# Retention heads inside the stick-breaking steps, roots by logarithm and exponential

## The reference, cut to what matters

```python
# block 2, retention: scores by a fixed decay, then a group norm per head and a gate
scores = einsum('bnihd,bnjhd->bnhij', qc, kc) * decay_intra
y_ret = head_group_norm(y_ret, ret_norm_gain) * silu(r_g)
# (yf - mu) * rsqrt(var + EPS), per head of 64, times gain
# block 2, stick-breaking
log_beta = log_sigmoid(z)
log_stay = where(mask, log_beta - z, 0.0)
log_w = log_beta + cumsum(log_stay, axis=3, reverse=True) - log_stay
w = where(mask, exp(log_w), 0.0);  y = einsum('bhqs,bhsd->bhqd', w, v)
mixed = concatenate([y_ret, rms_norm(y_sb)]) @ w_out
# peer
act = gelu(einsum('pd,ped->pe', xb, u[ids])) * gate
y = einsum('pe,ped->pd', act, v[ids])
```

## Time and profile before

| | us |
|---|---|
| median of 3 runs | 3147.92 (3145.39 to 3149.68) |
| the profiled execution | 3149.68 |
| its span | 3147.8 |
| PE busy | 3022.7 (96%) |
| DVE busy | 2420.9 (77%) |
| ACT busy | 1351.2 (43%) |
| POOL busy | 1356.0 (43%) |
| mean granted clock of PE | 0.982 |
| DMA | 931.22 MB, 296 GB/s mean |

### The profile page before, as it was taken

One profiled execution on the slowest core, in us unless ns is written; L12 is line 12 of the kernel. 1 busy time (PEld: TensorE's weight loads), 2 busy tenths in 40 slices (PEclk: granted clock), 3 DMA queues, 4 the chain that ended last, 5 costly groups with the idle time before them and its releaser, 6 DMA issues. The chain is left out here.

```text
span 3147.8 us, 45955 instructions
## 1 busy us (share of the span) xinstructions
PE 3022.7 (96%) x16392; PEld 2028.0 (64%) x16392; DVE 2420.9 (77%) x5361; ACT 1351.2 (43%) x3429; POOL 1356.0 (43%) x1066
## 2 busy tenths in 40 slices
PE   8999999899999999999999988998999999999998
PEld 3467488766666666666444564887666666666664
DVE  6885369989899888867733274699898998888777
ACT  3332222786666555510111172227866665555100
POOL 0000000767676776765300010006576767767654
PEclk9999999999999999999999999999999999999999
DMA  9511352999999999999822201619899999999998
GB/s 309 201 54 37 126 206 74 368 330 409 408 408 396 407 409 409 409 409 409 342 92 87 76 18 56 225 62 354 321 409 408 409 400 406 409 409 409 409 409 346
DMA packets 283115, 931.22 MB, mean 296 GB/s; under 512 B 31853, under 2 KB 32509, under 8 KB 282505
## 3 DMA queue, kind: packets, MB, share of 16 engines
q0 software_dynamic: 147840, 536.96, 43.3%
q1 hardware_dynamic: 135048, 391.34, 32.7%
HBM read 921.87 MB, written 6.32 MB: 295 GB/s over the span
## 5 line engine op out<-in xcount | busy, mean ns | idle before, releaser
L816 PE MATMUL psum<-hT,mod 128*128 128x256 f32 x4096 | 961.1, 389 | 7.3 <-ACT big L1364 6.3
L816 PEld LDWEIGHTS psum<-hT,mod 128*128 128x128 f32 x4096 | 777.4, 194 | 126.4 <-issue 26.1
L1374 ACT ACTIVATE levels<-key_numbers,hT 128x128 bf16<-128x128 f32 x1792 | 567.0, 389 | 245.8 <-PE psum L872 241.9
L2127 DVE SCALAR_TENSOR_TENSOR tmp<-w,small,tmp 128x1024 f32<-128x1024 f32 x339 | 435.7, 1285 | 92.6 <-DMA w<-in_peer_v,tmp 44.1
L2107 DVE CUSTOM_DVE_ANT_0 w<-w,hn 128x1024 f32<-128x1024 f32 x342 | 408.6, 1223 | 74.9 <-DMA w<-in_peer_down,tmp 39.0
L2307 POOL DMA_INDIRECT w<-in_peer_u,tmp x172 | 236.8, 1377 | 521.7 <-DVEq L1892 402.7
L826 PE MATMUL psum<-rows,big 128*128 128x512 f32 x752 | 337.1, 592 | 0.0
L872 PEld LDWEIGHTS psum<-x,levels 128*128 128x128 bf16 x6144 | 226.9, 103 | 165.9 <-issue 127.3
L1377 ACT ACTIVATE levels<-levels 128x512 bf16<-128x512 bf16 x448 | 282.3, 630 | 14.2
L2307 POOL DMA_INDIRECT w<-in_peer_down,tmp x170 | 235.2, 1384 | 119.5 <-DVE small L2107 78.0
L872 PE MATMUL psum<-x,levels 128*128 128x32 bf16 x6144 | 235.8, 196 | 52.4 <-DVE levels L1982 21.6
(11 more groups left out here) (358 smaller groups left out, 4205.6 us busy)
## 6 DMA issues: line engine op xcount, KB each, us to landing
mod<-in_uT SPq DMA_DIRECT2D x256, 512.0 KB
rows<-in_peer_v SPq DMA_DIRECT2D x64, 512.0 KB
rows<-in_peer_up SPq DMA_DIRECT2D x64, 512.0 KB
w<-in_w_in SPq DMA_DIRECT2D x14, 2048.0 KB, 8.0
srow<-in_peer_v SPq DMA_DIRECT2D x32, 512.0 KB, 7.1
tmp<-in_peer_v SPq DMA_DIRECT2D x32, 512.0 KB
srow<-in_peer_up SPq DMA_DIRECT2D x32, 512.0 KB, 6.8
tmp<-in_peer_up SPq DMA_DIRECT2D x32, 512.0 KB
```

Of the source, the lines that this page charges most:

```text
L816: last = nc.tensor.matmul(ps[4 + e % 2][:, 0:ND], ub[e % UV][:, k, :], hT[:, k, ND:SEQ], start=k == 0, stop=k == KC - 1)
L1374: last = nc.scalar.activation(hits[n % HITS][:, j * P:(j + 1) * P], keyno, ACT.Abs, bias=nibT[:, n * BATCH + j:n * BATCH + j + 1])
L2127: last = stt(y, row, c8[g % 2][:, b:b + 1], y, ALU.mult, ALU.add)
```

## The change

Three heads of retention (`AHEAD_HEADS`) stay ahead of the steps; the other five run inside the first 20: a step issues one key tile's scores after the stick scores, DVE multiplies by the decay at the end of its step, and PE sums a head's values at every fourth step. Their scores have two banks instead of four; retention's values and the sticks' share one bank, half each, with waits for its reading. Odd heads' keys get tiles of their own (`rk_odd`) whose other half POOL sets to zero. Weights and stays are stored as triangles, in `hT_`, `w_` and `top_`; for that reason SP loads the second half of w_out after the last step's sums, and the next section after the sticks' values and the scaling. Retention's norm goes by pairs of heads (`centred` at steps 1, 7, 15 and 23, squares, sums, one root at 27, `ret_normed` from 28 to 31, `gated` partly behind the steps); the gate times the gain is POOL's. A stick head's values are read one step earlier. One modulation product of 128x1024 on DVE moves from between retention heads to step 13. Every root is now `Exp(-0.5 * Ln(var))` without a reciprocal, and the table set that has both functions is loaded by name where it may be missing (the start, inside and after block 1's heads, after its late chunks, two places of its expert loop, and block 2 ahead of the first turns and of the steps). In the expert loops of both blocks `unit_gelu` stands ahead of `block_gelu` and `hit_batch`.

```diff
+AHEAD_HEADS = 3
...
+        rk_odd = [v.rearrange("p (g n) -> p g n", g=2) for v in (rows[:, 0, :], part(modm, 20, 4))]
...
-        stay = [part(big, 8 * n, 8).rearrange("p (j n) -> p j n", j=NT) for n in range(2)]
+        def triangle(base, at):
+            widths = [SEQ - j * P for j in range(NT)]
+            return [base[:, at + sum(widths[:j]):at + sum(widths[:j + 1])] for j in range(NT)]
+        stay = [triangle(w_, 1280 * n) for n in range(2)]
+        weights = [triangle(hT_, 1280 * n) for n in range(2)]
+        ret = [triangle(hT_, 2560), [top_[:, 0:512], top_[:, 512:896], w_[:, 3328:3584], w_[:, 3584:3712]]]
...
-        key_sums = [part(rows[:, 0, :], 2 * n, 1.5).rearrange("p (m n) -> p m n", m=3) for n in range(2)]
...
+            sp.wait_ge(ar_done, STICKS)
             load_section(25)
-            sp.wait_ge(pv_used, 8 + 16)
+            sp.wait_ge(pv_used, 8 + 8)
+            sp.wait_ge(src_ready, 9 * NT)
...
+            def ret_score(h, j):
+                n = h * NT + j
+                if n >= 2:
+                    pe.wait_ge(wt_ready, n - 1)
+                keys = rk_odd[h // 4][:, h // 2 % 2, :] if h % 2 else rkT[:, h // 2, :]
+                nc.tensor.matmul(ps[2 + n % 2][:, 0:SEQ - j * P], keys[:, j * P:(j + 1) * P], rqT[:, h // 2, j * P:SEQ],
+                                 start=True, stop=True).then_inc(ret_scored, 1)
+            def ret_values(h):
+                pe.wait_ge(wt_ready, (h + 1) * NT)
+                if h:
+                    pe.wait_ge(ret_used, h)
+                if h > AHEAD_HEADS:
+                    pe.wait_ge(pv_used, 8 + h - AHEAD_HEADS)
+                head_values(ps[0][:, 256:512], ret[h % 2], lambda j: rv[:, j, h * 64:(h + 1) * 64], ret_done)
+            pe.wait_ge(others_zeroed, 3)
+            for h in range(AHEAD_HEADS):
                 for j in range(NT):
-                    n = h * NT + j
-                    if n >= 4:
-                        pe.wait_ge(wt_ready, n - 3)
-                    nc.tensor.matmul(ps[4 + n % 4][:, 0:SEQ - j * P], rkT[prt, h // 2, j * P:(j + 1) * P],
-                                     rqT[prt, h // 2, j * P:SEQ], start=True, stop=True).then_inc(z_done, 1)
-                if h >= 1:
-                    pe.wait_ge(wt_ready, h * NT)
-                    values(h - 1, st1[(h - 1) % 2], lambda j: rv[:, j, (h - 1) * 64:h * 64], 64, first=h == 1)
-            pe.wait_ge(wt_ready, 8 * NT)
-            values(7, st1[1], lambda j: rv[:, j, 448:512], 64)
+                    ret_score(h, j)
+                if h:
+                    ret_values(h - 1)
...
+                if AHEAD_HEADS * NT + n < 8 * NT:
+                    ret_score(AHEAD_HEADS + n // NT, n % NT)
...
+                if n % NT == 1 and AHEAD_HEADS - 1 + n // NT < 8:
+                    ret_values(AHEAD_HEADS - 1 + n // NT)
...
-                nc.scalar.activation(std[:, at:at + n], var[:, at:at + n], ACT.Sqrt).then_inc(std_ready, 1)
+                root_step(nc.scalar.activation(lnv[:, at:at + n], var[:, at:at + n], ACT.Ln))
+                nc.scalar.activation(rs[:, at:at + n], lnv[:, at:at + n], ACT.Exp, scale=-0.5).then_inc(rs_ready, 1)
...
+                    nc.scalar.preload_act_table_set("natural_log_exp_and_others")
...
+                    for u in range(units_due(e - 2), units_due(e - 1)):
+                        unit_gelu(layer, u)
                     if EARLY <= e + AHEAD - 1 < NKEY:
                         block_gelu(layer, e + AHEAD - 1)
                     for n in range(batches_due(e) if e else 0, batches_due(e + 1)):
                         hit_batch(layer, 1 + n // BATCHES, n % BATCHES)
-                    for u in range(units_due(e - 2), units_due(e - 1)):
-                        unit_gelu(layer, u)
...
+                nc.scalar.activation(rk_odd[0][64:P, :, t * P:(t + 1) * P], bank[64:P, 0:2], ACT.Copy)
+                nc.scalar.activation(rk_odd[1][64:P, :, t * P:(t + 1) * P], bank[64:P, 2:4], ACT.Copy).then_inc(tr_free[n % 2], 1)
...
+            def ret_out(h):
+                act.wait_ge(ret_done, h + 1)
+                nc.scalar.activation(hn[:, :, h * 64:(h + 1) * 64], ps[0][:, 256:512].rearrange("p (t n) -> p t n", t=NT), ACT.Copy)\
+                    .then_inc(ret_used, 1)
...
-                if n in (2, 5, 8, 11):
+                if n in (1, 8, 16, 24):
+                    p = n // 8
                     seen.next(dve_to_act)
-                    act.wait_ge(heads_summed, 8 + n // 3)
-                    nc.scalar.activation(wide_sq, hn[:, n // 3, 0:512], ACT.Square).then_inc(ss_done, 1)
-                if n == 14:
+                    if p:
+                        act.wait_ge(ret_summed, p)
+                    nc.scalar.activation(wide_sq.rearrange("p (t n) -> p t n", t=NT), hn[:, :, p * P:(p + 1) * P], ACT.Square)\
+                        .then_inc(ss_done, 1)
+                if n == 26:
                     root(8 * NT)
-                    nc.scalar.preload_act_table_set("natural_log_exp_and_others")
...
-                    if j == 0 and h >= 1:
-                        head_out(h - 1, 64, 512, 8 + 8 + h, stick_sq[(h - 1) % 2], 8 + 4 + h - 2 if h >= 3 else 0)
-            head_out(7, 64, 512, 8 + 8 + 8, stick_sq[1], 8 + 4 + 6)
-            act.wait_ge(pv_used, 8 + 16)
+                    if j == 1 and h >= 1:
+                        head_out(h - 1, 64, 512, 8 + h, stick_sq[(h - 1) % 2], 8 + h - 2 if h >= 3 else 0)
+                if n % NT == 2 and AHEAD_HEADS - 1 + n // NT < 8:
+                    ret_out(AHEAD_HEADS - 1 + n // NT)
...
-                seen.next(std_ready)
-                step(nc.vector.reciprocal(rs[:, c], std[:, c]))
+                seen.next(rs_ready)
...
+            def ret_weights(h, j):
+                n = h * NT + j
+                if j == 0:
+                    dve.wait_ge(dec_in[h % 2], 16 * (h // 2 + 1))
+                    if h >= 2:
+                        dve.wait_ge(ret_done, h - 1)
+                dve.wait_ge(ret_scored, n + 1)
+                wd = SEQ - j * P
+                tt(ret[h % 2][j], ps[2 + n % 2][:, 0:wd], dec[h % 2][:, 0:wd], ALU.mult).then_inc(wt_ready, 1)
+            for h in range(AHEAD_HEADS):
+                for j in range(NT):
+                    ret_weights(h, j)
+            def centred(p):
+                pair = hn[:, :, p * P:(p + 1) * P].rearrange("p t (h n) -> p t h n", n=64)
+                mean = nt_[:, 0:8].rearrange("p (t h) -> p t h", h=2)
+                dve.wait_ge(ret_used, 2 * p + 2)
+                step(nc.vector.tensor_reduce(mean, pair, AX_X, ALU.add))
+                step(ts(nt_[:, 0:8], nt_[:, 0:8], 1.0 / 64, None, ALU.mult))
+                tt(pair, pair, mean.unsqueeze(3).to_broadcast([P, NT, 2, 64]), ALU.subtract).then_inc(dve_to_act, 1)
+            def ret_normed(t):
+                rv_, rshape = by_head(hn[:, t, 0:512], 8, 64)
+                step(tt(rv_, rv_, spread(rs[:, 8 * t:8 * t + 8], rshape), ALU.mult))
+            def gated(t):
+                dve.wait_ge(rg_ready, t + 1)
+                step(tt(hn[:, t, 0:512], hn[:, t, 0:512], rg[:, t, :], ALU.mult))
...
+            for n in range(STICKS + LOOK + 1):
+                if n in (1, 7, 15, 23):
+                    centred((n + 1) // 8)
+                if n in (2, 9, 17, 25):
+                    p = n // 8
+                    seen.next(ss_done)
+                    nc.vector.tensor_reduce(ss.rearrange("p (t h) -> p t h", t=NT)[:, :, 2 * p:2 * p + 2],
+                                            wide_sq.rearrange("p (t h n) -> p t h n", t=NT, n=64), AX_X, ALU.add).then_inc(ret_summed, 1)
+                if n == 13:
                     dve.wait_ge(mod_in, 16)
                     step(stt(rows[:, 1, :], mod[:, 4, :], 1.0, rows[:, 1, :], ALU.add, ALU.mult))
-                dve.wait_ge(dec_in[h % 2], 16 * (h // 2 + 1))
-                if h >= 2:
-                    dve.wait_ge(pv_done, 8 + h - 1)
-                for j in range(NT):
-                    n = h * NT + j
-                    dve.wait_ge(z_done, n + 1)
-                    wd = SEQ - j * P
-                    tt(st1[h % 2][:, j, j * P:SEQ], ps[4 + n % 4][:, 0:wd], dec[h % 2][:, 0:wd], ALU.mult).then_inc(wt_ready, 1)
-            def centred(t):
-                rv_, rshape = by_head(hn[:, t, 0:512], 8, 64)
-                mean = nt_[:, 0:8]
-                step(nc.vector.tensor_reduce(mean, rv_, AX_X, ALU.add))
-                step(ts(mean, mean, 1.0 / 64, None, ALU.mult))
-                tt(rv_, rv_, spread(mean, rshape), ALU.subtract).then_inc(dve_to_act, 1)
-                step(tt(rg[:, t, :], rg[:, t, :], srow[:, 0:512], ALU.mult))
-            def gated(t):
-                rv_, rshape = by_head(hn[:, t, 0:512], 8, 64)
-                step(tt(rv_, rv_, spread(rs[:, 8 * t:8 * t + 8], rshape), ALU.mult))
-                step(tt(hn[:, t, 0:512], hn[:, t, 0:512], rg[:, t, :], ALU.mult))
...
-            for n in range(STICKS + LOOK + 1):
```

(33 more changed lines are left out.)

83 lines of the change are left out of this document (50 added, 33 removed).

## The result

The changed kernel takes 3130.78 us (median of 6 runs, 3129.23 to 3134.83) against 3146.05 for the kernel before on the same chip (6 runs, 3144.53 to 3149.68): a ratio of 0.995, interval 0.994 to 0.996, some 15 us less. Forecast were 3136 us and a range of 3126 to 3147. The profiled execution has a span of 3128.7 us against 3147.8; of those 19.1 us some 4 belong to the profiled execution of before, which lay 3.6 us above its median.

What follows compares the result with a forecast made beforehand. Expert streams were taken as bound by bytes and matmul columns, retention by PE, the steps by PE, DVE and ACT together. Terms -26.9 + 14.0 - 1.9 + 1.3 + 0.5 + 1.0 gave -12.0 us: 3136 us, range 3126 to 3147.

Steps and rivals of the forecast that it cites:

- The stretch: Block 2, end of projections to first turn of the mixed tiles: ahead phase, steps and tail together, forecast -14.8 us.
- Ahead: Retention before the stick-breaking steps: three heads' scores and two heads' values stay, 12.3 us for 39.2, so -26.9 us.
- Steps: Stick-breaking steps with five heads' scores and six heads' values moved in: 93.6 us against 79.6, so +14.0 us.
- Tail: After the last sums: root loses table load and reciprocal, gains an activation, copies come earlier; -1.9 us.
- PE's 15.2 us of idle time: Old steps: 79.6 us less 64.4 of pure PE price, taken as idle; 1.5 + 3.5 us expected to stay.
- The first rival: Merged steps: the chain through DVE and ACT sets their pace, +8 us, 3144 us; chance 0.16.
- The 2.2 us a set: Merged steps: PE price per retention set of 1280 columns, engine taken as warm; 11 sets, 24.2 us.
- Block 1: Table set loaded by name between last late projection and first turn, where PE waits for ACT: +1.3 us.
- The two activations ahead of the queries: Start of both query phases, where PE waits for a root's chain: two activations for one, +0.5 us for both.
- The unit gelu: Expert loops: gathered unit's gelu ahead of the block gelu that PE waits for; +1 us, bounds -2.5 to +6.
- The third rival: Expert streams: unit gelu first frees gathered rows sooner, queues recover; 6 us a block, -24 in all, 3124 us; chance 0.05.
- The second, slower rival: Expert streams: PE's 10.4 us lost to the unit gelu are given back in neither block, +7.8, 3156 us; chance 0.08.

Runs made afterwards that it cites:

- experiment 6: Changed kernel with square root and reciprocal put back for every root, named table loads out; the stretch took 118.61 us against 115.98.
- experiment 3: Changed kernel with all eight retention heads ahead of the steps; 3136.08 us, ratio 0.9962, the stretch 120.39 us against 115.98.
- experiment 5: Changed kernel with eight heads ahead and retention's norm by pairs at the old kernel's steps; the stretch took 126.04 us against 120.39 with the new timetable.
- experiment 7: Kernel before with only the roots changed to exponential and logarithm; the stretch took 129.19 us against 131.29, one whole execution 3148.89 us.
- experiment 2: Kernel before with only the unit gelu moved ahead of block gelu and hit_batch; 3145.1 us, ratio 0.9991.
- experiment 8: Changed kernel with the gate times the gain back on DVE, none on POOL; the stretch took 115.99 us against 115.98.
- experiment 9: Changed kernel with block 1's table load moved from before the first turn to behind the second turned tile; 3132.39 us, ratio 0.9948.
- experiment 1: Changed kernel with the unit gelu put back behind block gelu and hit_batch in both expert loops; 3137.69 us, ratio 0.9969.
- experiment 11: Changed kernel with the unit gelu between block gelu and hit_batch in both expert loops; 3134.03 us, ratio 0.9954.
- experiment 12: Changed kernel with two heads ahead, six inside, centring at steps 4, 12, 20, 27, root at 31; the stretch took 116.36 us against 115.98.

## Why the prediction was right, and where it was not

The stretch was forecast to lose 14.8 us and lost 15.3. *Ahead*: 12.3 us said, 13.0 measured from the first retention score (1774.10) to the first stick score; the two banks cost short waits of 0.2 to 0.3 us each, and no wait on the decay tile came. *Steps*: 93.6 said, 93.54 measured, PE's work 88.6 said, 89.84 measured; as long as retention's scores ran the gaps were 0.24 us where 1.5 were allowed, behind them 3.5 (37.21 less 33.75), as allowed. So 1.2 us more work and 1.3 us less waiting cancel, which is luck. *Tail*: -1.9 said, -3.2 measured. The root's share is right to 0.1 us (experiment 6), the earlier copies gave 0.64 where 0.5 was said (a wait of 1.44 for 2.08 ahead of the last value product); the rest is that product, 1.2 us shorter by the clock, a term the sum did not have and luck in this execution. Without it the stretch loses 14.1.

The sum was right, and the reason for its largest term was not. It let retention's heads fill PE's 15.2 us of idle time. That figure is no idle time: the earlier trace rows has PE busy for 70.5 us of the steps, and the window cut at the last sums leaves 9.05 us of idle time, just the waits of the earlier trace rows. The other 6 us are PE at work for longer than the 64.4 us of the pure price, in part at the clock of 0.95 that stands in the same row. Experiments 3 and 5 show what most of the 9 us were: waits for DVE, crowded with the norm into the first 22 steps. Spreading the norm takes them from 8.0 to 4.5 us with no head moved. Moving five heads inside then lowers PE's idle time in the steps only from 4.8 to 3.7 us, and ahead of them from 3.0 to 1.8; the other 2.1 of its 4.4 us are shorter work (ahead and steps together 101.97 us busy in place of 104.10). The step that failed is the reading of the earlier trace rows: PE's waits for DVE were seen, and what kept DVE was not looked for in those steps.

The ledger of the stretch by the runs: moving five heads inside 4.4 us (experiment 3), the norm's timetable 4.5 in the steps (5), the roots 2.1 in the kernel before (7) or 2.6 in the changed one (6), the clock in the tail 1.2; together 12.2 to 12.7 of 15.3. The remaining 2.6 to 3.1 were not separated (the sticks' copies a step earlier, the triangles, scores over 128 rows from two banks). Part of them can be clock. In the kernel before, retention's last value product waits only 0.56 us and takes 3.74 us, where those ahead of it take 2.44 (timeline of PE):

```profile
1812.34 3.74 PE L966 MATMUL psum<-big,hT 128*128 128x64 f32 x20 [0.56 <-ACT hn L1178]
```

From there over the first stick scores the granted clock is 0.56; in experiment 5, with eight heads ahead as before, the same place has 1.00 (windows):

```profile
1812.34:1819.74 7.40, 7.40 (x31) 6.00 (x32) 0.93 (x3) 3.47 (x8) 0.00 (x0) 0.56 0.17 62
```

```profile
1811.04:1818.28 7.24, 7.24 (x57) 6.16 (x55) 3.47 (x10) 3.30 (x9) 0.45 (x1) 1.00 0.00 0
```

The clock falls there in the three profiles with the old retention (before, experiments 2 and 7) and in none of the eleven with the new one. By the first window that is up to 3.3 us (an estimate: 7.40 x 0.44). No run separates what in the new retention prevents it.

The first rival, DVE's chain setting the merged steps, is out: 56.09 of 56.33 us, and experiment 8.

Two smaller readings do not hold. The 2.2 us a set were taken because the engine is warm in the steps; the clock granted from 1776 to 1811 us, in retention, is 1.00 as well, so that is not why a set costs less among the sticks. And the bounds, added up, end at 3151 us, not 3146 (+3.7, +6.4 and +5 on the sum).

*Block 1* was to lose 1.3 us at the turn and lost 1.4 (1.81 for 0.39); the whole time did not show it (experiment 9). The two activations ahead of the queries were to cost 0.5 us and cost 0.46 (waits of 2.70 and 3.57 us become 2.93 and 3.80). Not foreseen: with logarithm and exponential in one set the softmax ahead of the first gelu finds its table there; the load at 522.62 us before has no counterpart after.

*The unit gelu* is the term with the wrong sign: +1 us in bounds of -2.5 to +6, and block 1 alone gave some 4: from the first expert product to the next projections it took 1043.6 to 1046.2 us in the three profiles with the unit behind both, 1039.3 to 1042.6 in the ten with it in front. Counted to the end of those projections, whose weights PE then waits for longer, it is 1251.8 to 1253.3 against 1247.3 to 1251.1 us, so some 2.6 on average stay. The mechanism was in the text, transfers of the stalled stream going to the gathers, and it was booked as a discount on PE's loss. The step that failed is the slack: the earlier trace rows has PE waiting for DVE at the end of block 1, where DVE itself stands behind gathered rows, which says that the gathered chain ends last there; then PE's loss is free, and what the gathers win is the gain. In the changed kernel that wait is gone, and PE waits a little for the stream's own rows instead (timeline of PE):

```profile
1551.34 1.13 PE L851 MATMUL psum<-tmp,big 128*128 128x512 f32 x2 [1.68 <-DMA tmp<-in_peer_v]
```

The third rival had its sign from the other end of the stream and was priced at 6 us a block. Its mechanism exists, since units run up to 13 us earlier in mid-stream than in experiment 1, but that lead is lost again by the end (experiment 11). The remark that nobody is seen to wait for that gelu was worth nothing: no wait names it in the changed kernel either, and its place moved the end of block 1 all the same. The second, slower rival did not come about: PE's waits on the block gelu grew from 6.3 us in all to 10.2, not by 10 in each block.

Of the two rules of the Trainium skill that the prediction names, the drain behind a table load ("ScalarE: Activation LUTs", "What ACT_TABLE_LOAD costs") does not show: taking the load from the tail gave 1.40 us with the reciprocal and the second activation accounted for, where the page's figures would give 2.8, an estimate. The contention of POOL and DVE over their SBUF interfaces (the Trainium skill, "GPSIMD Engine Reference", "1. Specifications", the row "SBUF interfaces") cost the stretch nothing that shows: 115.98 us with the gate's products on POOL, 115.99 without (experiment 8).

No variant was faster than the changed kernel by more than these runs can tell.

## What to carry to other kernels

Before idle time is filled with other work, look for whose time it is: list what the engine that is waited for did in those steps, and try to spread that first. When idle time is worked out as a span less the pure price of the work, set it beside the busy time and the clock of the same window: the rest can be slow work. Where two chains share the queues, find the one that ends last; a stall of the other can then pay instead of costing, as in block 1 here. And let the waits that a view names be one witness of several: no wait named the gelu whose place moved the end of block 1 by some 4 us.

## What the runs showed of the hardware

PE's clock at the same place differs between executions that are otherwise alike. At the start of block 1's queries PE has waited 2.70 to 2.94 us in all fourteen profiles; the first 32 products then took 7.14 us in five of them and 8.53 to 10.20 in the others. The changed kernel and that of experiment 1 at this point, PE's timeline:

```profile
395.40 7.14 PE L814 MATMUL psum<-hT,big 128*128 128x256 f32 x32 [2.93 <-ACT hT L1186]
```

```profile
395.37 8.83 PE L814 MATMUL psum<-hT,big 128*128 128x256 f32 x32 [2.93 <-ACT hT L1186]
```

and their windows from 395 to 400 us, granted clock 1.00 and 0.67 of the upper level of 2.4 GHz:

```profile
395.00:400.00 5.00, 4.60 (x21) 4.10 (x22) 1.90 (x4) 0.57 (x2) 0.00 (x0) 1.00 1.05 408
```

```profile
395.00:400.00 5.00, 4.63 (x14) 3.88 (x15) 1.87 (x4) 0.16 (x1) 0.00 (x0) 0.67 1.05 409
```

So 1.7 us can come or go behind a wait of 3 us, with nothing seen in these profiles that says when, as much as the edit of experiment 9 was worth. The tail is the same: after the same wait of 1.44 us the last value product took 2.44 us in the changed kernel, 3.04 in experiment 11 and 3.56 in experiment 5, and after 2.08 us it took 3.62 us before and 2.42 in experiment 2. How busy PE was in the steps does not decide it: in experiment 12 it was busy for 93.83 of 96.02 us, and the product took 3.74.
